# Split output product in the RWKV layer of a three-layer network on one Trainium2 core: high and low pieces, 512 columns a pass

## The reference, cut to what matters

```python
    y = rwkv7_scan(rh, hs(decay), kh, vh, kk, hs(a))
    ...
    y_a = ((y + bonus.reshape(b, t, D_RWKV)) * g.astype(f32)).astype(h.dtype)
    ...
    conv = lax.conv_general_dilated(glu, conv_w[:, None, :], ...) + conv_b
    y_b = jax.nn.silu(layer_norm(conv, conv_ln_g, conv_ln_b, CONV_LN_EPS))
    return jnp.concatenate([y_a, y_b], axis=-1) @ w_out
    ...
        x = x + rms_norm_2(m, g[3])
        f = swiglu(rms_norm_2(x, g[4]), ffn_w_gate[layer, 1], ffn_w_up[layer, 1], ffn_w_down[layer, 1])
```

## Time and profile before

| | us |
|---|---|
| median of 3 runs | 1823.32 (1823.17 to 1823.38) |
| the profiled execution | 1821.56 |
| its span in the profile | 1819.7 |
| PE busy | 1787.7 (98%) |
| DVE busy | 1203.8 (66%) |
| ACT busy | 910.8 (50%) |

### The profile page before, as it was taken

How to read it: one execution, slowest core, us unless ns; L and a number is a source line. 1 busy time by engine, 2 the same in 40 slices (tenths; PEclk the granted TensorE clock), 3 DMA queues, 4 the chain that set the end, 5 groups by cost and what they waited for, 6 DMA issues and landing times.

```text
span 1819.7 us, 25089 instructions
## 1 busy us (share of the span) xinstructions
PE 1787.7 (98%) x10394; PEld 1514.8 (83%) x10394; DVE 1203.8 (66%) x1512; ACT 910.8 (50%) x1123; POOL 54.7 (3%) x97
## 2 busy tenths in 40 slices
PE   8999999999999999999999999999999999999998
PEld 7998898888888887888888898888888878788887
DVE  5347678789888898555478956554754567875554
ACT  4345453577767676444322335444544446654443
POOL 0040000000000001000000000000100000000000
PEclk9999999999999999999999999999999999999999
DMA  9343344699989897655333008545545544236550
GB/s 366 131 171 117 116 144 154 247 349 361 343 342 345 326 352 291 233 187 186 113 142 113 26 17 307 185 173 197 208 176 194 188 159 166 89 142 240 185 181 27
DMA packets 51520, 363.53 MB, mean 200 GB/s; under 512 B 5712, under 2 KB 5840, under 8 KB 8784
## 3 DMA queue, kind: packets, MB, share of 16 engines
q1 hardware_dynamic: 51264, 359.83, 53.5%
q10 hardware_dynamic: 144, 2.10, 0.3%
HBM read 360.86 MB, written 1.05 MB: 199 GB/s over the span
## 4 chain that ended last, share of the span: by engine, by line
PE 91%; DVE 6%; ACT 2%; issue 1%; DMA 0%; POOL 0%; DVEq 0%; SPq 0%; POOLq 0%; ACTq 0%
PE bank L3012 8%; PE bank L3014 8%; PE bank L3013 8%; PE bank L2484 8%; PE bank L3039 4%; PE bank L3037 4%; PE bank L3038 4%; PE bank L2542 4%; PE bank L2866 3%; PE bank L2868 3%; PE bank L2867 3%; PE bank L2674 3%; PE bank L2883 2%; PE bank L2885 2%; PE bank L2884 2%; PE bank L3333 2%
## 5 line engine op out<-in xcount | busy, mean ns | idle before, releaser
L1487 DVE TENSOR_TENSOR w_a<-ring,w_a 128x2048 fp32r<-128x2048 f32 x220 | 501.7, 2290 | 271.7 <-ACT w_a L888 270.6
L888 ACT ACTIVATE w_a<-ring 128x2048 fp32r<-128x2048 f32 x220 | 418.1, 1912 | 171.7 <-PE bank L3039 90.1
L1487 DVE TENSOR_TENSOR w_b<-ring,w_b 128x2048 fp32r<-128x2048 f32 x63 | 144.2, 2289 | 72.9 <-ACT w_b L888 72.6
L3012 PE MATMUL bank<-w_a,h 128*128 128x512 f32 x464 | 183.5, 395 | 0.5 <-DVE w_a L1487 0.5
L3014 PE MATMUL bank<-w_a,h 128*128 128x512 f32 x464 | 181.0, 390 | 0.0
L3013 PE MATMUL bank<-w_a,h 128*128 128x512 f32 x464 | 180.6, 389 | 0.0
L888 ACT ACTIVATE w_b<-ring 128x2048 fp32r<-128x2048 f32 x63 | 120.5, 1913 | 51.6 <-PE bank L3039 27.8
L2484 PE MATMUL bank<-h,w_a 128*128 128x256 f32 x1088 | 143.0, 285 | 1.2 <-DVE ring_lo L1588 1.0
L2484 PEld LDWEIGHTS bank<-h,w_a 128*128 128x128 f32 x1088 | 134.5, 191 | 4.4 <-issue 3.4
L1225 ACT ACTIVATE sil<-bank,tiny 128x256 f32<-128x256 f32 x88 | 41.8, 474 | 174.2 <-PE bank L3014 174.2
L3037 PE MATMUL bank<-w_a,hid 128*128 128x512 f32 x280 | 109.8, 392 | 0.0
(11 more groups left out here) (534 smaller groups left out, 3448.7 us busy)
## 6 DMA issues: line engine op xcount, KB each, us to landing
ring<-in_stream SPq DMA_DIRECT2D x330, 1024.0 KB, 4.9
G<-in_gains SPq DMA_DIRECT2D x15, 512.0 KB, 5.7
cmp_area<-in_cmp_w ACTq DMA_DIRECT2D x1, 2048.0 KB, 11.3
sm<-in_small SPq DMA_DIRECT2D x1, 1582.0 KB, 13.3
con<-in_consts SPq DMA_DIRECT2D x1, 1032.0 KB, 17.2
X<-in_x SPq DMA_DIRECT2D x2, 512.0 KB, 4.9
out_x<-X SPq DMA_DIRECT2D x4, 256.0 KB, 2.0
sm<-in_small SPq DMA_DIRECT2D x1, 730.5 KB, 23.6
```

The lines of the kernel that those rows point to most:

```text
L888: act.activation(w_slot(unit)[:, 0, :], ring[:, unit % RING, :], ACT.Copy).then_inc(S("w_hi"), 1)
L1487: dve.tensor_tensor(w_slot(unit)[:, 1, :], ring[:, unit % RING, :], w_slot(unit)[:, 0, :].bitcast(FP32), ALU.subtract).then_inc(S("w_lo"), 1)
L3012: pe.matmul(bank[4 + t][:, :], x_hi, w[0][:, k, :], start=first, stop=False)
```

## The change

The output matrix of mixer ab is now laid out in half-row units (512 output columns x 512 input channels each), split into high and low pieces by ACT and DVE, as are the mixed activations; `out_part` makes three products of 512 columns for each 128 input channels where it made two of 256 (at full float) for the same output. PE's order in the product changes: the convolution's first half for both token tiles comes first. ffn1 and ffn2 go through the four slots in another order, (2, 1, 0, 3). With it these PREV values change: ffn1's units 0, 2 and 3 wait for ffn0+29, ab_out+3 and ab_out+2 (ffn0+31, ffn0+29 and ffn0+30 before), c+0 for ffn2+31 (ffn2+29 before) and c+2 for ffn2+29 (ffn2+31 before); c+1 and c+3 keep theirs.

The convolution's bias is added, doubled, in the first tap, and four scalings after the last tap are gone (the norm's epsilon is four times as large instead). One product of 8 heads (`per_head(bank[7], 0, 1, ...)`) and the last `mw_in` stand elsewhere in PE's order. At the start the second tile of x is loaded ahead of the gains; ACT makes unit 0's high piece between the two tiles' copies; PE has 5 dummy products instead of 16 and runs the first unit as one pass over high x high, low x high and high x low, with a wait for each.

```diff
-    units += list(column_units(a["ab_w_out_2"][0]))
+    units += [half_row_units(a["ab_w_out_2"][0])[n] for n in (1, 3, 0, 2)]
...
                 if name == "c":
                     s = 2 + n if n < 2 else (n - 2) % SPLIT
+                if name in ("ffn1", "ffn2"):
+                    s = (2, 1, 0, 3)[place % SLOTS]
+                    if name == "ffn1" and s in (0, 3) and n < SLOTS:
+                        in_slot[s] = D_UNITS["ab_out"] + (3 if s == 0 else 2)
...
+        AB_PARTS = ("u0", "u1", "u2", "c0", "c1", "r0", "u3", "r1")
+        mixed_hi, mixed_lo = merged_lo, f_hi[:, :, :].rearrange("p t (k n) -> p (t k) n", k=4)
+        def blend_unit(n):
+            unit = D_UNITS["ab_out"] + n
+            return unit, (w_a[:, 0, 1, :], y_2[:, :, :].rearrange("p a n -> p (a n)"), w_b[:, 0, 1, :], w_a[:, 0, 0, :])[n]
...
             sp.dma_start(X[:, 0, :], x[0:P, :]).then_inc(S("x"), 16)
+            sp.dma_start(X[:, 1, :], x[P:T, :]).then_inc(S("x2"), 16)
             load_gain(0, 1)
-            sp.dma_start(X[:, 1, :], x[P:T, :]).then_inc(S("x2"), 16)
...
-            for t in range(TT):
-                turned_in("proj", t)
-            for n in range(2):
-                split("proj", n)
+            turned_in("proj", 0)
+            split("proj", 0)
+            turned_in("proj", 1)
+            split("proj", 1)
...
             shifted_in(5)
+            def mixed_high(part):
+                if part[0] == "u":
+                    unit, high = blend_unit(int(part[1]))
+                    act.wait_ge(S(f"unit{unit % RING}"), 16 * (unit // RING + 1))
+                    act.activation(high, ring[:, unit % RING, :], ACT.Copy).then_inc(S("gate_hi"), 1)
+                else:
+                    ks, tok = ab_part(part)
+                    act.activation(mixed_hi[:, ks, tok], H[:, ks, tok], ACT.Copy).then_inc(S("gate_hi"), 1)
+            mixed_high("u0")
             for n in range(N_INV):
...
             solution_out(0)
+            act.wait_ge(S("mw_full"), N_INV)
+            mixed_high("u1")
...
+            link(dve.tensor_scalar(twice_b, P2("conv_b"), 2.0, None, ALU.mult))
...
-                    for m in range(MT):
-                        ins = dve.tensor_scalar(cacc[:, m, :], cacc[:, m, :], 0.5, P2("conv_b")[:, m:m + 1], ALU.mult, ALU.add)
-                    ins.then_inc(S("ln_dve"), 1)
...
+            def mixed_low(part):
+                dve.wait_ge(S("gate_hi"), ab_at(part))
+                if part[0] == "u":
+                    unit, high = blend_unit(int(part[1]))
+                    ins = dve.tensor_tensor(ring_lo[:, unit % RING, :], ring[:, unit % RING, :], high.bitcast(FP32), ALU.subtract)
+                else:
+                    ks, tok = ab_part(part)
+                    ins = dve.tensor_tensor(mixed_lo[:, ks, tok], H[:, ks, tok], mixed_hi[:, ks, tok].bitcast(FP32), ALU.subtract)
+                ins.then_inc(S("gate_lo"), 1)
...
-            keep_busy(16, 4)
-            pe.wait_ge(S("h_lo"), 4)
+            keep_busy(5, 4)
+            pe.wait_ge(S("w_hi"), 1)
...
                 if n == N_INV - 1:
                     solve(0)
+                    mw_in(N_INV - 1)
                     pe.wait_ge(S("ln_dve"), AT["ln_conv"])
...
+                    ps = sums[2 * t + n][:, :]
+                    pe.matmul(ps, x_hi, high, start=(k == MT), stop=False)
+                    pe.matmul(ps, x_hi, low, start=False, stop=False)
+                    ins = pe.matmul(ps, x_lo, high, start=False, stop=(k == MT - 1))
                 return ins
             turn_mixed(0)
...
+            for t in range(TT):
+                for n in range(2):
+                    out_part(t, n, range(MT, MT + 2))
+            for n in range(2):
+                out_part(0, n, range(MT + 2, KD))
+            turn_mixed(1)
+            out_part(0, 0, range(MT))
+            out_part(0, 1, range(MT)).then_inc(S("sums_0"), 1)
+            for n in range(2):
+                out_part(1, n, range(MT + 2, KD)).then_inc(S("unit_used"), 1)
+            out_part(1, 0, range(MT)).then_inc(S("unit_used"), 1)
+            out_part(1, 1, range(2))
+            x_turn("ffn1", 0)
+            out_part(1, 1, range(2, MT)).then_inc(S("unit_used"), 1)
```

More of the change, by code:

```diff
@@ L593, in out_unit @@
             unit = D_UNITS["c_out"] + n
-            return unit, w_a[:, 2 - 2 * (n // 2), n % 2, :], len(MG_ITEMS) + len(OUT_HI) + n + 1
+            return unit, w_a[:, 2 - 2 * (n // 2), n % 2, :], len(MG_ITEMS) + len(OUT_HI) + len(AB_PARTS) + n + 1
         OUT_HI, OUT_LO = (("u0", "u1", "p0", "u2", "p1", "p2", "u3", "p3"), ("u0", "u1", "p0", "u2", "p1", "p2", "p3", "u3"))
@@ L900, in post_square @@
                 elif half == 0 and by_half(name, t):
-                    act.wait_ge(S("unit_used"), D_UNITS[SUMS[name][0]] + 2)
+                    act.wait_ge(S("unit_used"), D_UNITS[SUMS[name][0]] + (3 if name == "ffn1" else 2))
                 elif half == 0 or by_half(name, t):
@@ L2576, in _ @@
                 x_turn("proj", t)
-            keep_busy(16, 4)
-            pe.wait_ge(S("h_lo"), 4)
-            for name in ("u0", "u1", "v0", "v1", "ga0", "ga1", "re0", "re1", "q0", "q1", "kvc"):
+            keep_busy(5, 4)
+            pe.wait_ge(S("w_hi"), 1)
+            first_w, first_ps = parts(D_UNITS["proj"], KD), group_begin("u0")
+            for a, (wp, x, ready) in enumerate(((0, h_hi, "h_hi"), (0, h_lo, "h_lo"), (1, h_hi, None))):
+                if ready is None:
+                    lo_ready(D_UNITS["proj"])
+                for k in range(KD):
+                    if ready is not None and k % 4 == 0:
+                        pe.wait_ge(S(ready), HI0["proj"] + 3 + k // 4)
+                    for c in range(2):
+                        ins = pe.matmul(first_ps[:, c * T:(c + 1) * T], first_w[wp][:, k, c * P:(c + 1) * P], x[:, k, :],
+                                        start=(a == 0 and k == 0 and c == 0), stop=(a == 2 and k == KD - 1 and c == 1))
+            ins.then_inc(S("unit_used"), 1)
+            for name in ("u1", "v0", "v1", "ga0", "ga1", "re0", "re1", "q0", "q1", "kvc"):
                 (split_tokens if name[0] == "v" else split_channels)(group_begin(name), "proj", FULL[name][1] - 1)
@@ L3327, in out_part @@
             def out_part(t, n, ks):
-                w = unit_ready(D_UNITS["ab_out"] + n)
                 for k in ks:
-                    if n == 0 and t == 0 and k >= MT:
-                        pe.wait_ge(S("y_conv"), k - MT + 1)
-                    ins = pe.matmul(sums[2 * t + n // 2][:, (n % 2) * UC:(n % 2 + 1) * UC], H[:, k, t * P:(t + 1) * P], w[:, k, :],
-                                    start=(n % 2 == 0 and k == MT), stop=(n % 2 == 1 and k == MT - 1))
+                    unit, high = blend_unit(n + 2 * (k < MT))
@@ new lines, in out_part @@
+                    if k >= MT:
+                        pe.wait_ge(S("gate_lo"), ab_at(f"c{(k - MT) // 2}"))
+                    elif t == 0:
+                        pe.wait_ge(S("gate_lo"), ab_at("u3" if n else "r0"))
+                    else:
+                        pe.wait_ge(S("gate_lo"), ab_at("r1"))
+                    high, low = (w.rearrange("p (k n) -> p k n", k=4)[:, k % 4, :] for w in (high, ring_lo[:, unit % RING, :]))
+                    x_hi, x_lo = (x[:, k, t * P:(t + 1) * P] for x in (mixed_hi, mixed_lo))
@@ L3345, in _ @@
-            ins.then_inc(S("sums_0"), 1)
-            for n in range(SQUARE):
-                out_part(1, n, range(MT, KD))
-                if n == 0:
-                    pe.wait_ge(S("y_rw"), 2)
-                out_part(1, n, range(MT)).then_inc(S("unit_used"), 1)
-                if n == 1:
-                    x_turn("ffn1", 0)
+            for t in range(TT):
[3 more added lines that the diff above has]
+                out_part(0, n, range(MT + 2, KD))
```

49 lines of the change are left out of this document (35 added, 14 removed).

## The result

The changed kernel takes 1826.85 us (median of 13 runs, 1825.96 to 1827.99) against 1822.0 for the kernel before in the same runs: a ratio of 1.0024, interval 1.0016 to 1.0032, slower by 3 to 6 us. The forecast was 1826.5, in a range of 1822.9 to 1829.5.

What follows compares the result with a forecast made beforehand. PE was taken to bound the kernel (busy 98%, the chain on it for 91% of the span). Terms -3.0 + 1.2 - 1.7 + 6.7 = +3.2 us took the median 1823.32 to 1826.5, range 1822.9 to 1829.5.

Steps and rivals of the forecast that it cites:

- The start: -3.0: Program start to the projection: earlier loads and unit 0's earlier high piece save 3.0 us; bounds -1.8 and -3.6.
- The half rate that was to cost 0.6: Projection's first products: with 5 dummies instead of 16 they fall into PE's slow time, losing 0.6 us.
- Round 0: +1.2: Inverse's first round: ACT's high piece of the first output unit delays its copies and PE by 1.2 us; bounds 0.5, 1.4.
- End of ab: -1.7: End of mixer ab and ffn1's start: shorter product, less waits and norms, saves 1.7 us; bounds -2.3 and +0.5.
- state 2.0: End of mixer ab: PE waits 2.0 us for DVE's state, because two low pieces come before the centring.
- low piece 0.9: Mixer ab's end: the first product waits for the activations' high and low piece, +0.9 us.
- norm of tile 0 0.8: Mixer ab's output product: 0.8 us of wait for tile 0's norm, as its pieces make DVE and ACT late.
- `turned_in` 1.8: ffn1's start: ACT's copies of tile 0 stand behind ffn1+1's piece, and PE waits 1.8 us.
- `ffn1+2`: ffn1's start: ACT's piece of this unit comes after the output product, 1.8 us ahead of the square starting tile 1's norm.
- For the clock I add 0.6: End of mixer ab: 0.6 us, because the new state wait may do what the old lull did (1.65).
- c+0's wait: +6.7: End of ffn2, start of mixer c: c+0 waits for ffn2+31, delaying mixer c's transposes by 6.7 us; bounds 5.5, 8.4.
- The clock falls in the new wait: Rival, chance 0.12: clock falls behind the wait before `down_last(1)`, in mixer c's first products, costing 1.7 us: +4.9, 1828.2.

Runs made afterwards that it cites:

- before_start: The kernel before with only the change's edits at the start (second x tile first, early high piece, 5 dummies, one-pass first unit): 1819.72 us, ratio 0.9988.
- c_slots: The changed kernel with slots 0 and 2 exchanged from mixer c on, so c+0 again waits for ffn2+29: 1819.52 us, ratio to the kernel before 0.9982.
- ab_alone: The changed kernel with the old kernel's start and slots 0 and 2 exchanged from mixer c on, leaving mixer ab's rewriting: 1823.13 us, ratio 1.0003.
- no_dummies: The changed kernel without the 5 dummy products behind the first transposes: 1827.47 us, ratio to the kernel before 1.0023.
- two_products: The changed kernel without the output product's third product (low activations by high matrix), 64 instructions instead of 96: 1827.33 us, ratio to the kernel before 1.0027.
- u0_late: The changed kernel with ACT's high piece of the first output unit moved behind the inverse's last round: 1826.52 us, ratio to the kernel before 1.002.
- combined_u0_late: The changed kernel with c's slots exchanged, DVE's state earlier, ACT's ffn1+2 piece behind tile 1's square, u0's high piece behind the inverse: 1818.02 us.
- before_rotation: The kernel before with only the slot rotation (2, 1, 0, 3) of ffn1 and ffn2: 1829.36 us, ratio 1.003.

## Why the prediction came out as it did

**The sum.** The time was right to 0.4 us, and part of that is luck. Against the profiled execution before, 3.2 us were forecast and 5.9 came. Of the missing 2.7, 2.3 lie in mixer ab and 0.3 at mixer c. By the medians the change cost 4.85 us (1822.0 to 1826.85); the forecast of 1826.5 met it because it started from 1823.32, the median of three runs, 1.3 us over that of the thirteen. The kernel before spreads that much by itself: at a mean clock of 0.999 it took 1820.0 to 1821.9, at 0.998 mostly 1823.0 to 1823.5, at 0.997 1824.7 to 1825.2, and the profiled one (1821.56) had a fall of 3.4 us. The largest chance, 0.49, went to a difference within 0.2%, and the ratio is 1.0024.

**The start: -3.0, right and a little small.** -2.99 in the changed kernel's trace, -3.1 to -4.4 in the eight others with the same start and no fall ahead. The half rate that was to cost 0.6 cost 0.1 to 0.3: the first 48 products took 6.0 to 6.2 where 5.9 is full rate. Where the second tile of x landed early, they began at 13.4 to 13.7; in the changed kernel's trace, at 14.30.

**Round 0: +1.2, right.** PE's wait is 1.20 and the loss against the kernel before was 1.1 at that place. What was missing is the next limit: taken away, the gain is met by an "issue" wait of 1.0 to 1.35 us (1.07 in before_start, where nothing delays round 0).

**End of ab: -1.7, wrong in the clock.** The list of waits was right: state 2.0 (measured 1.64), low piece 0.9 (0.9 where no clock fell), norm of tile 0 0.8 (0.26), `turned_in` 1.8 (1.36), and `ffn1+2` (0.58, of which 0.3 came back when the order was mended). The product took 0.232 us an instruction, not 0.227 (21 from 1075.23 to 1080.10), from 1071.88 to 1096.2 with its transposes. The 215.8 ns that the prediction takes from the Trainium skill (TensorE: Matmul & The Clock Gate, Back-to-back issue gap) are that page's figure for a single product by itself; no run here shows them.

The step that failed is "For the clock I add 0.6": the wait for the state brought 6.8 us at 0.50 where the old kernel had 3.4. Over the middle stretch, -0.5 was forecast (1.2 - 1.7); without a fall it is -0.34 (c_slots), with 6.8 us +1.84, with 10.2 us +2.9 (ab_alone). So 3.4 us at 0.50 cost 0.8 to 1.1 here (0.8 by no_dummies), not 1.7: of the 3.3 us that the products lost in the changed kernel's trace, 0.9 came back because the wait for the low piece behind them is filled.

The -0.34 flatters the change, for the kernel before had its fall in this stretch and c_slots had none. What that fall cost can be estimated from before_start, the old code without a fall: 98.53, less its "issue" wait of 1.07, is 97.46, 1.4 us under the 98.89 with the fall. At the full clock on both sides the rewriting of mixer ab is then 1.1 us slower (98.55 against 97.46, an estimate), where the prediction's terms without those for the clock make it 0.55 (1.2 - 1.7 + 1.65 - 0.6). Of the 2.3 us, 0.5 are thus waits and rates that came out a little larger, and 1.8 the clock: forecast as -1.05 (-1.65 + 0.6), measured as +0.75 (2.18 - 1.43).

**c+0's wait: +6.7, right.** 7.04, and 6.78 with the rotation alone. The wait of 5.0 against 4.9 and the room of 2.5 against 2.6 are as worked out. (A slip on the way: 1474.2 and twice 0.69 are 1475.6 and not 1475.4, which would give +6.8.) "The clock falls in the new wait", the rival with 0.12, was right in what happens and wrong in what it costs: the fall came (6.8 us), which the prediction had named as a sign of being wrong, and the norm hid it. The rule behind it (the Trainium skill, TensorE: Matmul & The Clock Gate, What's actually happening: the throttled state is the default) agrees with the trace as far as the fall goes, behind a wait of 5.0 us and behind one of 1.64, though in c_slots none came behind the same 1.64; the 1828.2 that was hung on it did not come.

**Where the output product's 5.8 us went.** 128 instructions of 0.216 us (27.6 us, from the prediction) became 96 of 0.232, 5.3 us less, and the stretch got 0.3 us shorter at best, which is less than the fall of the kernel before had cost. 1.64 went into the state, 1.20 into round 0, 0.9 into the low piece where no clock fell, 1.36 into the copies behind ffn1+1's piece, and 0.26 and 0.58 into the norms. In two_products another 32 instructions less brought nothing in the median, and 4.3 us more of such waits.

## What to carry to other kernels

When slots or buffers rotate in a new order, write down for every unit which unit had its place last and when that one is released, in the stages that the edit doesn't name too: the largest term here (+7.0 us) came from a mixer that was not touched, and relabelling two slots removed it (PE's wait was gone, and the time fell by 7.3). On an engine that works strictly in order, look at what is queued behind a new wait: the copy of the hidden tile needed 0.4 us and was 5 us late. Making PE's work shorter is worth something only where PE's chain sets the end; take a third of it away and see, before rewriting it.

## What the runs showed of the hardware

In the traces the granted clock fell to 0.50 behind lulls of PE of 1.0 to 5 us, for 3.4, 6.8 or 10.2 us, and not in every execution of the same code: behind waits of 1.02, 1.13 and 1.64 us it fell in one trace and not in another, and behind the 5.0 us before `down_last(1)` it fell in all that left that wait empty. In the kernel before it fell behind the inverse's last rounds, which are small products of 64 columns with waits of up to 0.75 us between them. From run to run the kernel before, unchanged, had a mean granted clock from 0.997 to 0.999, and its times follow it over 5 us (1820.0 to 1825.2). With products in the lull (dummies) the clock did not fall there in the one trace at the state and the one at mixer c, and by the mean clock of the other runs it mostly did not at the state. At the start PE runs at 0.5 to 0.6 of its later rate for some time while the windows show a granted clock of 1.00, as in no_dummies, where both stretches hold the same kind of product (13 in the first 2.5 us, 21 in the second):

```profile
14.00:16.50 2.50, 2.50 (x13) 2.50 (x13) 2.50 (x2) 1.53 (x1) 0.00 (x0) 1.00 0.99 422
16.50:19.00 2.50, 2.50 (x21) 2.50 (x20) 2.46 (x2) 0.00 (x0) 0.00 (x0) 1.00 1.01 424
```

In before_start, u0_late and combined_u0_late PE waited 1.0 to 1.35 us and DVE 1.5 to 1.9 us for nothing that an engine releases ("issue"), PE always after the eleventh of the same 16 transposes. In these three the program started 3.1 to 3.9 us earlier than the kernel before and the first round of the inverse ran undelayed; the kernel before and before_rotation, undelayed too but with the old start, have no such wait.
